# Marks of the experts' second index in one VectorE operation, the gates multiplied on by ScalarE, gelus a tile later

## The reference, cut to what matters

```python
# for every token: 8 heads x 16 experts = 128 pairs (i, j) out of 128 x 128 experts, each with a gate
act  = gelu(einsum('td,thkd->thk', h, expert_u[expert_idx]))
coef = gate * act
out  = einsum('thk,thkd->td', coef, expert_v[expert_idx])
```

## Time and profile before

| | |
|---|---|
| median of 3 runs | 2676.93 us |
| span of the profiled execution | 2674.9 us |
| PE, DVE, ACT, POOL busy in the span | 89%, 67%, 30%, 46% |
| token stage | 1676.85 to 2006.90 us |
| passes in it | 48 |

### The profile page before, as it was taken

The page is one execution under the profiler, slowest core; times in us unless marked ns, Lnnn a source line. Parts: engine busy times, 40 slices in busy tenths (PEclk is TensorE's granted clock), DMA queues, the critical chain, the costliest instruction groups (busy, mean ns, idle before and its releaser), DMA issues.

```text
span 2674.9 us, 36953 instructions
## 1 busy us (share of the span) xinstructions
PE 2383.4 (89%) x12641; PEld 2016.9 (75%) x12641; DVE 1779.8 (67%) x3319; ACT 793.6 (30%) x1164; POOL 1229.1 (46%) x681
## 2 busy tenths in 40 slices
PE   6898888988988899994999969989998999999995
PEld 2686776867767767773899969889998777777774
DVE  3566465664655621115457799878873799999999
ACT  3313222132122213222333424333332333333331
POOL 0303123021130213441444769555557777777773
PEclk8998998989989899997999989998999999999998
DMA  5201001011010012222334768687779988888884
GB/s 208 94 17 47 31 31 63 16 47 39 24 63 31 32 64 95 94 102 73 123 121 132 241 200 286 237 313 293 266 288 384 382 327 325 325 327 326 325 327 147
DMA packets 146945, 459.29 MB, mean 172 GB/s; under 512 B 14273, under 2 KB 47169, under 8 KB 145729
## 3 DMA queue, kind: packets, MB, share of 16 engines
q1 hardware_dynamic: 107760, 291.78, 31.1%
q0 software_dynamic: 36864, 134.23, 13.5%
q10 hardware_dynamic: 2256, 32.51, 3.0%
HBM read 403.94 MB, written 54.53 MB: 171 GB/s over the span
## 4 chain that ended last, share of the span: by engine, by line
PE 51%; DVE 21%; issue 14%; DMA 7%; POOL 3%; ACT 3%; DVEq 1%; SPq 0%; ACTq 0%; POOLq 0%
PE bank L520 9%; PE bank L521 9%; PE bank L522 9%; DVE pair L1509 6%; DMA rows<-peer_u,e_row 4%; DVE cv L1132 3%; PE pair L1692 3%; PE bank L1707 2%; PE bank L1700 2%; DVE c_lo L1496 2%; PE bank L1937 2%; POOL w_lo L926 2%; DVE dY L1170 2%; PE bank L1633 1%; PE bank L1567 1%
## 5 line engine op out<-in xcount | busy, mean ns | idle before, releaser
L926 POOL TENSOR_TENSOR w_lo<-raw,w_hi 128x1024 fp32r<-128x1024 f32 x208 | 504.2, 2426 | 908.4 <-ACT w_hi L663 533.9
L520 PE MATMUL bank<-lat_hi,w_hi 128*128 128x384 f32 (+1 forms) x1536 | 563.0, 367 | 30.0 <-ACT gu L838 9.7
L521 PE MATMUL bank<-lat_lo,w_hi 128*128 128x384 f32 (+1 forms) x1536 | 547.9, 357 | 0.0
L522 PE MATMUL bank<-lat_hi,w_lo 128*128 128x384 f32 (+1 forms) x1536 | 547.8, 357 | 0.0
L926 POOL TENSOR_TENSOR w_lo<-raw_more,w_hi 128x1024 fp32r<-128x1024 f32 x136 | 328.9, 2419 | 196.8 <-ACT w_hi L774 115.7
L520 PEld LDWEIGHTS bank<-lat_hi,w_hi 128*128 128x128 f32 x1536 | 293.9, 191 | 51.2 <-issue 32.1
L1490 DVE TENSOR_TENSOR cf<-gl,gq 128x384 f32<-128x384 f32 x128 | 321.3, 2510 | 11.6 <-DMA gq<-g_dram 6.1
L522 PEld LDWEIGHTS bank<-lat_hi,w_lo 128*128 128x128 f32 x1536 | 292.5, 190 | 21.7
L521 PEld LDWEIGHTS bank<-lat_lo,w_hi 128*128 128x128 f32 x1536 | 293.6, 191 | 17.5
L1956 PE MATMUL bank<-w_hi,c_hi 128*128 128x512 f32 x768 | 251.0, 408 | 4.3 <-DVE c_lo L1496 4.2
L1956 PE MATMUL bank<-w_hi,c_lo 128*128 128x512 f32 x768 | 239.4, 393 | 0.0
(11 more groups left out here) (342 smaller groups left out, 3896.4 us busy)
## 6 DMA issues: line engine op xcount, KB each, us to landing
raw<-w SPq DMA_DIRECT2D x208, 512.0 KB, 3.8
raw_more<-w SPq DMA_DIRECT2D x136, 512.0 KB, 4.2
gu_dram<-gu SPq DMA_DIRECT2D x128, 192.0 KB, 4.7
g_dram<-gs ACTq DMA_DIRECT2D x6, 4096.0 KB, 16.4
gl<-gu_dram SPq DMA_DIRECT2D x16, 1536.0 KB, 10.8
gq<-g_dram SPq DMA_DIRECT2D x16, 1536.0 KB, 11.9
ada<-w_ada SPq DMA_DIRECT2D x32, 512.0 KB, 4.0
ada_a<-w_ada SPq DMA_DIRECT2D x8, 512.0 KB, 9.0
```

The costliest lines, as they stand in the source:

```text
L520: nc.tensor.matmul(out, hi, rh, start=start, stop=False)
L521: nc.tensor.matmul(out, hi, rl, start=False, stop=False)
L522: return nc.tensor.matmul(out, lo, rh, start=False, stop=stop)
L926: nc.gpsimd.tensor_sub(w_lo[:, slot, :], raw_at(slot % 2 if src is None else src), w_hi[:, slot, :].bitcast(F32)).then_inc(split_done, 1)
```

## The change

Three things are changed together:

1. VectorE makes the marks of index j for four tokens in one `tensor_tensor` (128x512), as it does for i, in place of four `tensor_scalar` (128x128) that also multiplied by the gate. Both mark operations count on one semaphore, `marked`. The dots of two groups all stand behind the odd group.
2. ScalarE multiplies the gates on: eight `activation(Copy, scale=gate)` of 128x128 in each pass, in place, at the head of its pass, each four behind a wait for `marked`; they count on `weighted`, and TensorE waits for that.
3. In ScalarE's queue each gelu, and the high part with it, comes a tile later: in a pass the copies stand first, then the gelu of the pass before and the high part that belongs to it. So that this works, the last tile of every block of the candidate stage is left to the next block, and its exponential stands one tile earlier.

The diff:

```diff
--- before.py
+++ after.py
@@ -461,8 +461,8 @@
         g2_mm = sem("g2_mm")
         g2_ev = sem("g2_ev")
         h2_tok = sem("h2_tok")
-        oh_i_done = sem("oh_i_done")
-        oh_j_done = sem("oh_j_done")
+        marked = sem("marked")
+        weighted = sem("weighted")
         g_mm = sem("g_mm")
         g_ev = sem("g_ev")
         gs_st = sems("gs_st", 2)
@@ -849,18 +849,19 @@
                     act.wait_ge(s_mm, i * 4 + (j + 1))
                     nc.scalar.copy(sc[:, j % 2, :, :].rearrange("p a b -> p (a b)"), bank[4 + j % 2][:, :]).then_inc(s_ev, 1)
 
-            def soft(b):
+            def soft(b, first=False):
 
                 for j in range(U_CD):
-                    act_u(b, U_CD, X_CD + j)
-                    hi_n(T_U + RING + j, b, U_CD)
+                    if j or not first:
+                        act_u(b, U_CD, X_CD + j - 1)
+                        hi_n(T_U + RING + j - 1, b, U_CD)
                     if j == 8:
                         act.wait_ge(cd, b * CD_N + CD_EXP)
                         nc.scalar.activation(bf[5][:, :, :], bf[4][:, :, :], ACT.Exp).then_inc(cd_exp, 1)
 
             act.wait_ge(s_ev, 2 * PH)
             nc.scalar.copy(bank[5][:, 0:P], iota).then_inc(e_free, 1)
-            soft(0)
+            soft(0, True)
             with act.Fori(1, LAT) as b:
                 soft(b)
                 act.wait_ge(e_tr, b)
@@ -873,14 +874,22 @@
                     with act.Fori(0, GTOK // 32) as t:
                         for w in range(4):
                             for z in range(2):
+                                q = j * GTOK // 4 + 2 * w + z
+                                act.wait_ge(marked, i * (GTOK) + t * 16 + (2 * q + 2))
+                                for v in range(4):
+                                    col = bass.ds(i * (2 * GTOK) + t * 32 + (4 * q + v), 1)
+                                    own = hole_j[:, 4 * z + v, 0:P]
+                                    nc.scalar.activation(own, own, ACT.Copy, scale=eidT[:, 2, col]).then_inc(weighted, 1)
+                            for z in range(2):
                                 act.wait_ge(g_mm, i * (2 * GTOK // 4) + t * 8 + (j * GTOK // 4 + 2 * w + z + 1))
                                 nc.scalar.copy(gs[:, j, :, bass.ds(t * 32 + (8 * w + 4 * z), 4)],
                                                bank[z][:, :].rearrange("p (t i) -> p i t", t=4)).then_inc(g_ev, 1)
                             x = i * (2 * GTOK // 8) + t * 4
-                            act.wait_ge(a_mm, x + (X_G + j * (GTOK // 8) + w + 1))
-                            act.wait_ge(gu_st[w], x * 4 + (X_G + j * (GTOK // 8) + w) // 4 * 16)
-                            nc.scalar.activation(gu[:, w, :], bank[6 + w % 2][:, 0:DT], ACT.Gelu).then_inc(gelu, 1)
-                            n = T_U + X_G - 2 * PH + j * (GTOK // 8) + RING + w
+                            own_x = X_G + j * (GTOK // 8) + w - 1
+                            act.wait_ge(a_mm, x + (own_x + 1))
+                            act.wait_ge(gu_st[own_x % 4], x * 4 + own_x // 4 * 16)
+                            nc.scalar.activation(gu[:, own_x % 4, :], bank[6 + own_x % 2][:, 0:DT], ACT.Gelu).then_inc(gelu, 1)
+                            n = T_U - 2 * PH + own_x + RING
                             act.wait_ge(raw_full[raw_slot(n)], x * 4 + raw_loads(n) * 16)
                             nc.scalar.copy(w_hi[:, n % RING, :], raw_at(raw_slot(n))).then_inc(hi_done, 1)
                     act.wait_ge(g_ev, i * (2 * GTOK // 4) + (j + 1) * (GTOK // 4))
@@ -891,7 +900,7 @@
                 nc.scalar.copy(c_hi[:, y % 4, :], cf[:, y % 2, :]).then_inc(ch, 1)
 
 
-            for x in range(X_END, PK):
+            for x in range(X_END - 1, PK):
                 if x == PK - 4:
                     for j in range(2):
                         act.wait_ge(gs_st[j], DT // GTOK // 2 * 16)
@@ -1460,11 +1469,9 @@
                 own = slice(4 * z, 4 * z + 4)
                 cols = bass.ds(i * 128 + 4 * g, 4)
                 nc.vector.tensor_tensor(hole_i[:, own, 0:P], rep(bank[5][:, 0:P], 4), bc(eidT[:, 0, cols], P),
-                                        ALU.is_equal).then_inc(oh_i_done, 1)
-                for v in range(4):
-                    col = bass.ds(i * 128 + (4 * g + v), 1)
-                    nc.vector.tensor_scalar(hole_j[:, 4 * z + v, 0:P], bank[5][:, 0:P], eidT[:, 1, col], eidT[:, 2, col],
-                                            ALU.is_equal, ALU.mult).then_inc(oh_j_done, 1)
+                                        ALU.is_equal).then_inc(marked, 1)
+                nc.vector.tensor_tensor(hole_j[:, own, 0:P], rep(bank[5][:, 0:P], 4), bc(eidT[:, 1, cols], P),
+                                        ALU.is_equal).then_inc(marked, 1)
 
             dve.wait_ge(e_free, LAT)
             def token_block(i, first):
@@ -1473,8 +1480,9 @@
                     if g >= 2 or not first:
                         dve.wait_ge(g_mm, i * 32 + (g - 1))
                     marks(i, g)
-                    for m in range(DOT_T * g // 8, DOT_T * (g + 1) // 8):
-                        dot(i, DOT_G + m)
+                    if g % 2:
+                        for m in range(DOT_T * (g - 1) // 8, DOT_T * (g + 1) // 8):
+                            dot(i, DOT_G + m)
 
             token_block(0, True)
             with dve.Fori(1, DT // P) as i:
@@ -1929,8 +1937,7 @@
             with pe.Fori(0, DT // 32) as i:
                 for w in range(4):
                     for z in range(2):
-                        pe.wait_ge(oh_i_done, i * 8 + (2 * w + z + 1))
-                        pe.wait_ge(oh_j_done, i * 32 + (8 * w + 4 * z + 4))
+                        pe.wait_ge(weighted, i * 32 + (8 * w + 4 * z + 4))
                         if z == 0:
                             pe.wait_ge(g_ev, i * 8 + 2 * w)
                         for v in range(4):
```

## The result

| | us, median | range, runs |
|---|---|---|
| before | 2678.27 | 2673.47 to 2684.88, 20 |
| changed | 2684.73 | 2677.68 to 2690.17, 20 |
| predicted | 2695 | 2652 to 2710 |

The ratio is 1.0019, with a 95% interval of 1.0010 to 1.0027: the change costs 5 to 6.5 us, about as much as the prediction called the least that can be told (5.4). The sign was right and the size was not: +18.2 us were forecast for the span, and the profiled spans differ by 7.5 (2674.9 and 2682.4).

What follows compares the result with a forecast made beforehand. The prediction took TensorE as the bound, with five passes delayed by late rows behind stores. Terms +15.5, +0.7, +3, +1, -2 and 0 gave +18.2 on 2674.9, so 2693.1, and with 2.0 for the median 2695 us, range 2652 to 2710.

Steps and rivals of the forecast that it cites:

- the five events: Token-stage passes disturbed after stores of G: each to cost 10.6 us in place of 7.5, +15.5 in all.
- What bounds the kernel: Token stage: TensorE bounds undisturbed passes of 5.95 us; five passes delayed by late rows lose 37.6 of 44.5 us.
- VectorE's part: Token-stage marks: new operation 0.68 us, a pass's VectorE work 1.3 us shorter, worth nothing by itself in undisturbed passes.
- ScalarE's part: Token-stage gates: 0.41 us long, 0.31 apart; they fit before TensorE wants them, with 0.2 us to spare.
- the gates are too slow: Token stage: gates 0.41 us apart make TensorE wait 0.5 us every pass, +24 on the forecast, 2712 us; chance 0.12.
- The move in the queue: ScalarE's queue, token stage: high part begun 2.4 us later, gather 6.8 after its pass's start, store 3.6 earlier against TensorE.
- VectorE's shorter pass doesn't help: Token-stage passes behind a store: marks wait for a row in DRAM, not for VectorE, so its saved 1.3 us gains nothing.
- First marks: Start of the token stage: 1.29 + 1.34 us in place of 1.96 until TensorE can start, +0.7.
- The early wait: Token stage near 1700: a gather issued 2.4 us later loses 5.3 plus 0.6 in place of 2.9, +3.
- Candidate stage: Last gelu of a block waits behind transposed indices, but its low part is needed four tiles later: 0.
- nothing moves: Token stage: late-row passes stay at 7.5 us because the earlier store also ends earlier; 2677 to 2682 us, chance 0.15.
- The second rival: Token stage: stalls behind stores vanish, 37.6 us less, 2639 us; or shorten, 2654 us; chance 0.23.

Runs made afterwards that it cites:

- b_early: The kernel before with the token stage's gathers issued one tile earlier on GpSimd: 2632.18 us, ratio 0.9850.
- a_early2: The changed kernel with the token stage's gathers issued two tiles earlier: 2635.97 us, ratio to the kernel before 0.9852.
- own_pass: The kernel before with parts 1 and 2 but not part 3, each gelu and high part in its own tile's pass: 2861.32 us, ratio 1.0662.
- late_only: The kernel before with part 3 alone, marks and gates staying on VectorE: 2717.58 us, ratio 1.0150.
- a_delay: The changed kernel with each store of G issued behind the first pass of the next block: 2687.46 us, ratio to the kernel before 1.0035.
- a_cand: The changed kernel with the candidate stage's gelus in their old places, the shift beginning with its last tile: 2682.71 us, ratio to the kernel before 1.0016.

## Why the prediction was wrong, point by point

The direction was right, by the small terms alone, and most of the working too. What failed is the largest term of the sum, the price of the five events: the row's landing was taken as 13.4 us behind its gather's issue, and it was 11.65 in the first event.

- **What bounds the kernel** held: TensorE in the undisturbed passes, and five late rows behind stores for nearly all the rest. When the rows come in time TensorE is not idle at all from 1720 to 1965 (b_early, a_early2), and 46 us go against the kernel before (b_early), 49 against the changed one (a_early2).
- **VectorE's part** held: 681 ns for the new mark operation, and passes of 5.95 us as before.
- **ScalarE's part** held: 398 ns for a product, eight in 2.46 us, 0.29 apart (0.41 and 0.31 had been taken), and no stall for gates where no row is late. The rival "the gates are too slow" is out. own_pass shows how narrow the place for them is.
- **The move in the queue** held in every position: the gather 6.8 us behind its pass's start and 3.8 behind the store. That part 3 costs by itself, 40 us, is shown by late_only.
- **The five events failed: the term 5 x (10.6 - 7.5) = +15.5 was 0.** The step was "Behind a store it takes 14.2 (the row), or 12.7 if it lands with the store (16.4 - 3.7) ... I take 7.8". The landing was counted from the gather's issue, with figures from a store that takes 16.4 us. But the row follows the store's landing, and the store is not always 16.4 us: it is 13.9 in the changed kernel, where one gather goes out just ahead of it, and moving the store and the gathers against each other had changed the pair of the earlier trace rows (1727.19 and one 1.3 behind it, store at 1729.46) into a single one (1733.35, store at 1735.50). In the first event the row came 11.65 us behind its issue instead of 13.4, which is 1.75 of the 7.8; TensorE was itself 0.85 late by then (it reached 1745.25, and 1732.51 + 2 x 5.95 is 1744.4); the way from the dot to the product is 5.1 and not 5.4. 7.8 - 1.75 - 0.85 - 0.3 = 4.9, measured 4.83. The 2.8 for the clock held there. a_delay bears the first of these out: in its profiled execution, with the long store back in four of the five events, the same 41 passes lose 7.7 us more, half of the missing 15.5. The other half goes with TensorE's being late already and the shorter way behind the dot (1.15 us in the first event); no run tests it by itself. The crossing of one and two gathers was seen in four kernels and swapped by one tile's shift in both directions. Whether it is the gathers ahead of the store or the whole pattern of gathers around it that counts was not separated. Why it lengthens the store by 2.5 us is not settled; about 1.1 of it is that the store's first record starts later, on average 3.0 us behind the issue in the kernel before and 1.8 in the changed one.
- **"VectorE's shorter pass doesn't help"** was half right. It doesn't bring the row. But against late_only, whose row comes as late, the events make TensorE wait 5.2 and not 8.5 us. A likely reason, not tested alone, is that with the j marks in one operation per group and the dots behind both groups, more marks stand ready when VectorE begins to wait. The working had this in it (the row was wanted 12.4 us after the pass's start), it is only now that its worth is known: 3.3 us an event.
- **First marks** +0.7: measured +0.9. **The early wait** +3: 11.52 and 6.87 between gelus are 6.5 over two passes, 2.9 before, so +3.6. **Second of two gathers** +1: it lies in the 0.5 to 0.9 us ahead of some events and isn't separate.
- **Behind the stage** -2: measured -0.7. **Candidate stage** 0: about +2. The working looked at when TensorE needs the low part and forgot GpSimd, in whose queue gathers stand behind it. The trace of a_cand, where the late row and the 2.3 us are gone, bears this out.
- With the events at 0, the terms of the prediction give 18.2 - 15.5 = +2.7; the candidate stage adds 2, the rest of the tail 1.3, and 6.0 stand against a measured +5 to +7.5. The rival "nothing moves", 2677 to 2682, had the event's size right and its reason half: the store does end earlier against TensorE, but the 3.6 us of its earlier issue were in the forecast already, and it took a store 2.5 us shorter as well, which no term and no rival had. That losses and gains of the events cancel so nearly is luck of where the gathers fall, not a merit of the change.
- The second rival's 2639 leaves out the 2.0 us between span and median that the other figures have; 2641 is right. This changes no range.

## What to carry to other kernels

In these kernels a row whose gather goes out some 4 us behind a large store in another queue lands just behind that store, here 0.9 to 2.1 us behind its last record, up to 3.5 in a_delay: count such a landing from the store's issue and the store's length, and look for what the edit puts just ahead of the store. Before pricing a change to an engine's work, ask what a late transfer costs in each pass and try the cheap cure first; here one number in the table of gathers was worth 46 us, and the rearranged marks and gates cost 5. Where an engine's queue is short of slack, count the issues in it as work: what stands behind them decides.
